# Router logits from x with scaled weights, h shared with GpSimd beside the top-k, and squares and fill work reordered

## What is computed

```python
h = rmsnorm(x) * gain * (1 + scale) + shift       # per channel; scale, shift differ for context and latent tokens
aff = softmax(h @ w_router)                       # over 16 experts
g, idx = top_k(aff.T, cap)                        # 16 context and 32 latent tokens for each expert
hid = silu(h[idx] @ w_gate) * (h[idx] @ w_up)
out = (hid @ w_down) * g                          # scattered back by idx
```

## Time and profile before

| | us |
|---|---|
| median of three runs | 2028.72 |
| lowest, highest | 2028.66, 2030.94 |
| the profiled execution, its own time | 2027.77 |
| its span in the profile | 2025.7 |
| PE busy | 1867.7 (92%) |
| DVE, ScalarE, GpSimd busy | 592.7, 341.0, 60.4 |
| HBM read | 546.91 MB |

### The profile page before, as it was taken

One profiled execution on the slowest core, in us unless ns is written; L12 is line 12 of the kernel. 1 busy time (PEld: TensorE's weight loads), 2 busy tenths in 40 slices (PEclk: granted clock), 3 DMA queues, 4 the chain that ended last, 5 costly groups with the idle time before them and its releaser, 6 DMA issues.

```text
span 2025.7 us, 19626 instructions
## 1 busy us (share of the span) xinstructions
PE 1867.7 (92%) x8214; PEld 938.6 (46%) x8214; DVE 592.7 (29%) x1160; ACT 341.0 (17%) x787; POOL 60.4 (3%) x47
## 2 busy tenths in 40 slices
PE   5999999999999988888789999999999998888886
PEld 2565556555544333233345655565555343333323
DVE  1232447545221111101132324654533102010102
ACT  4022331100211101000141322210003010100102
POOL 1100000000000000000030000000000000000000
PEclk9999999999999999999999999999999999999998
DMA  9322272442589999999972221716225999999995
GB/s 389 152 94 88 84 307 78 166 166 77 208 365 428 429 429 429 430 429 428 426 309 94 83 88 57 287 42 249 110 102 245 396 429 428 429 429 428 429 429 243
DMA packets 53544, 552.38 MB, mean 273 GB/s; under 512 B 5840, under 2 KB 10832, under 8 KB 12240
## 3 DMA queue, kind: packets, MB, share of 16 engines
q1 hardware_dynamic: 49680, 548.51, 65.2%
q10 hardware_dynamic: 3776, 2.62, 0.4%
HBM read 546.91 MB, written 4.19 MB: 272 GB/s over the span
## 4 chain that ended last, share of the span: by engine, by line
PE 65%; DMA 29%; DVE 3%; ACT 2%; issue 1%; POOL 0%; SPq 0%; POOLq 0%; DVEq 0%; ACTq 0%
PE psum L943 12%; DMA ring<-in_w_up 12%; PE psum L1115 12%; DMA ring<-in_w_down 12%; PE psum L802 11%; PE psum L1027 6%; PE psum L804 6%; PE psum L1040 4%; DMA wide<-in_w_gate 3%; PE psum L397 2%; DMA ring<-in_w_gate 2%; PE psum L862 1%; PE psum L765 1%; PE psum L1095 1%; PE psum L1163 1%
## 5 line engine op out<-in xcount | busy, mean ns | idle before, releaser
L943 PE MATMUL psum<-hT,ring 128*128 128x384 f32 x768 | 255.8, 486 | 0.0
L802 PE MATMUL psum<-hT,ring 128*128 128x384 f32 x720 | 244.4, 493 | 7.2 <-ACT dense L1295 5.1
L1115 PE MATMUL psum<-dense 128*64 128x512 f32 x864 | 195.4, 596 | 30.8 <-DMA dense<-in_w_up 17.6
L1115 PE MATMUL psum<-ring,dense 128*64 128x512 f32 x832 | 188.2, 596 | 26.9 <-DMA ring<-in_w_gate 16.0
L943 PEld LDWEIGHTS psum<-hT,ring 128*128 128x128 f32 x768 | 145.7, 190 | 100.9
L802 PEld LDWEIGHTS psum<-hT,ring 128*128 128x128 f32 x720 | 135.8, 193 | 96.5 <-issue 6.6
L1115 PEld LDWEIGHTS psum<-dense 128*64 128x64 f32 x864 | 62.5, 137 | 153.6 <-issue 129.1
L1027 PE MATMUL psum<-dense,ring 128*128 128x384 f32 x384 | 131.9, 487 | 0.0
L1805 DVE TENSOR_TENSOR state<-state,psum 128x512 f32<-128x512 f32 x32 | 22.0, 688 | 373.2 <-PE psum L1115 335.2
L804 PE MATMUL psum<-ring,hT 128*128 128x512 f32 x288 | 126.5, 592 | 0.0
L1115 PEld LDWEIGHTS psum<-ring,dense 128*64 128x64 f32 x832 | 59.8, 137 | 140.7 <-issue 119.1
(11 more groups left out here) (211 smaller groups left out, 1680.2 us busy)
## 6 DMA issues: line engine op xcount, KB each, us to landing
ring<-in_w_up SPq DMA_DIRECT2D x32, 2048.0 KB, 38.2
ring<-in_w_in SPq DMA_DIRECT2D x60, 1024.0 KB, 8.6
dense<-in_w_up SPq DMA_DIRECT2D x30, 2048.0 KB, 40.0
ring<-in_w_down SPq DMA_DIRECT2D x30, 2048.0 KB, 40.1
dense<-in_w_gate SPq DMA_DIRECT2D x24, 2048.0 KB, 35.6
wide<-in_w_down SPq DMA_DIRECT2D x20, 2048.0 KB, 40.2
ring<-in_w_gate SPq DMA_DIRECT2D x20, 2048.0 KB, 36.7
wide<-in_w_gate SPq DMA_DIRECT2D x20, 2048.0 KB, 38.1
```

The costliest lines, as they stand in the source:

```text
L802: last = M.matmul(psum[:, bank, 0:T], ring[:, n % RING, k, cols], hT[:, k, :], start=k == 0, stop=k == KD - 1)
L943: last = M.matmul(psum[:, Z[1], 0:T], ring[:, n_gate % RING, k, (j % 4) * P:(j % 4 + 1) * P], hT[:, k, :], start=k == 0, stop=k == KD - 1)
L1115: last = M.matmul(psum[HALF * half:HALF * (half + 1), bank, :], lhsT(k), w[:, kk, half * SLAB:(half + 1) * SLAB], start=k == 0, stop=k == ...
```

## The change

- Router: the logits are computed from xT and not from hT. DVE scales the router weights by the modulation's scale (router_scaled, one copy for context and one for latent columns). PE multiplies them with the chunks of xT, chunks 0 to 3 inside w_out (after group 5) and 4 to 7 after the norm sum; DVE multiplies the result by rs, which is the inverse norm of each token. The part of the logits that comes from the shift is made from w_r and modT (eight two-column products after group 1 of w_out), spread with a product with ones into PSUM, and the gather adds to it.
- The first chain fill moves from right behind w_out to behind the gathered logits. The other fills move behind the transposes of the affinities.
- h: DVE normalises chunks 0 to 2, between steps of the softmax. GpSimd normalises chunks 3 to 7 and applies scale and shift to chunks 6 and 7. ScalarE applies them to chunks 0 to 5, in between its reads of fills. The transposes of hT come in two halves (chunks 0 to 3, 4 to 7) after those of the affinities.
- Squares: three buffers, and GpSimd adds four chunks, not six. PE sums chunks 4 to 6 directly, then GpSimd's sum, then chunk 7. This holds for all five norm sums.
- Starts: in layer 0 w_in 0 is in ring slot 3 and modulation slab 3 in slot 0, half a z group comes before the transposes of modulation slab 1, and four z groups are begun ahead and not three. In layer 1 a modulation product comes before the norm sum, and two z groups are begun ahead.
- Decays: DVE computes their logarithms before rotation 2 and ScalarE makes the exponentials behind its reads of z groups 4, 5 and 6.
- keep_busy has 4 dummy products beside the top-k, where layer 0 had 8 and layer 1 had 18.

The core of the diff; context is cut, blocks are moved to the left, the semaphores' declarations are left out, and so are the decay blocks that only move.

```diff
-ADDED = 6
-DVE_MODULATES = ((3, 6, 7), (6, 7))
+ADDED = 4
+BEGUN = (4, 2)
+DVE_MODULATES = ((3, 6, 7), ())
+DVE_NORMS = 3
...
+router_scaled = flat(state1).rearrange("p (g k e) -> p g k e", g=2, k=KD)
+router_shift = w_r[:].rearrange("p k e -> p (k e)")[:, 0:NBLK * NE].rearrange("p (g e) -> p g e", g=NBLK)
...
-[("mod", 1, 1), ("modT", 1, 1), ("mod", 1, 3), ("modT", 1, 3)]]
+[("mod", 1, 1), ("mod", 1, 3), ("modT", 1, 1), ("modT", 1, 3)]]
...
-SLABS = [[("mod", j) for j in START_MODS[l]] + [("w_in", j) for j in range(9)] + [("mod", j) for j in DENSE_MODS[l]]
+FIRST_SLABS = [[("mod", 0), ("mod", 2), ("mod", 1), ("w_in", 0), ("mod", 3)], [("mod", 1), ("mod", 3), ("w_in", 0)]]
+SLABS = [FIRST_SLABS[l] + [("w_in", j) for j in range(1, 9)] + [("mod", j) for j in DENSE_MODS[l]]
          + [x for b in range(3) for x in (("w_in", 9 + 2 * b), ("branch", b), ("w_in", 10 + 2 * b))] + [("w_out", 0), ("w_out", 1)]
...
+load_half(0, 3, 0)
 wait_slab_free(sp, 0, 0)
-load_half(0, RING, 0)
-load_slab(0, 3)
-load_half(0, RING, 1)
+load_slab(0, RING)
+load_half(0, 3, 1)
...
-G.tensor_tensor(sum_sq, square[:, 0, :], square[:, 1, :], ALU.add).then_inc(sq_added, 2)
+G.tensor_tensor(sum_sq, squared[0], squared[1], ALU.add).then_inc(sq_added, 2)
 for k in range(2, ADDED):
     pool.wait_ge(sq_added, at(sq_added, mixer * ADDED + k))
     pool.wait_ge(sq_ready, at(sq_ready, mixer * KD + k + 1))
-    G.tensor_tensor(sum_sq, sum_sq, square[:, k % 2, :], ALU.add).then_inc(sq_added, 1)
+    G.tensor_tensor(sum_sq, sum_sq, squared[k % 3], ALU.add).then_inc(sq_added, 1)
...
 add_squares(layer, 1)
+pool.wait_ge(rs_ready, at(rs_ready, 2))
+for k in range(DVE_NORMS, KD):
+    G.tensor_tensor(hT[:, k, :], xT[:, k, :], rs[:], ALU.mult).then_inc(norm_pool, 1)
+for k in POOL_MODULATES:
+    pool.wait_ge(norm_pool, at(norm_pool, k - DVE_NORMS + 1))
+    for g, cols in enumerate((CTX, LAT)):
+        last = G.tensor_scalar(hT[:, k, cols], hT[:, k, cols], scale_ffn_all[:, layer, k, g:g + 1],
+                               modT_all[:, layer, 24 + k, g:g + 1], ALU.mult, ALU.add)
+    last.then_inc(h_pool, 1)
...
-pe.wait_ge(sq_added, count(sq_added, (mixer + 1) * ADDED))
-M.matmul(psum[:, bank, 0:T], ones, sum_sq, start=True, stop=False)
 for k in range(ADDED, KD):
+    if k == KD - 1:
+        pe.wait_ge(sq_added, count(sq_added, (mixer + 1) * ADDED))
+        M.matmul(psum[:, bank, 0:T], ones, sum_sq, start=False, stop=False)
     pe.wait_ge(sq_ready, count(sq_ready, mixer * KD + k + 1))
-    last = M.matmul(psum[:, bank, 0:T], ones, square[:, k % 2, :], start=False, stop=k == KD - 1)
+    last = M.matmul(psum[:, bank, 0:T], ones, squared[k % 3], start=k == ADDED, stop=k == KD - 1)
     last.then_inc(sq_summed, 1)
...
-    fill(START_FILL[0][1:6])
+    fill(START_FILL[0][1:5])
     z_first_half(0)
+    fill(START_FILL[0][5:6])
     z_first_half(1)
     fill(START_FILL[0][6:7])
     z_first_half(2)
     fill(START_FILL[0][7:8])
+    z_first_half(3)
 else:
+    fill(START_FILL[layer][0:1])
     norm_sum(TR[0], 0)
-    fill(START_FILL[layer][0:1])
+    fill(START_FILL[layer][1:2])
     z_first_half(0)
-    fill(START_FILL[layer][1:3])
+    fill(START_FILL[layer][2:4])
     z_first_half(1)
...
+def router_part(chunks):
+    pe.wait_ge(w_read, at(w_read, chunks[-1] + 1))
+    for g, cols in enumerate((CTX, LAT)):
+        for k in chunks:
+            q = k % 4
+            last = M.matmul(psum[32 * q:32 * q + 32, (O[0], TR[1])[g], cols], router_scaled[:, g, k, :], xT[:, k, cols], start=k < 4, stop=k >= 4)
+    return last
...
 for j in range(KD):
     if j % 4 == 0:
...
+    if j == 1:
+        pe.wait_ge(router_in, at(router_in, 16))
+        pe.wait_ge(mod2_ready, at(mod2_ready, 1))
+        pe.wait_ge(co_read, at(co_read, 4))
+        for k in range(KD):
+            q = k % 4
+            last = M.matmul(psum[32 * q:32 * q + 32, O[0], 0:2], w_r[:, k, :], modT_all[:, layer, 24 + k, :], start=k < 4, stop=k >= 4)
+        last.then_inc(shift_full, 1)
+    if j == 5:
+        pe.wait_ge(router_ready, at(router_ready, 2))
+        pe.wait_ge(shift_read, at(shift_read, 1))
+        router_part(range(4))
+norm_sum(TR[0], 1)
+router_part(range(4, KD)).then_inc(lgT_full, 1)
+pe.wait_ge(shift_ready, at(shift_ready, 3))
+M.matmul(psum[:, O[1], 0:NBLK * NE], ones, router_shift.rearrange("p g e -> p (g e)"), start=True, stop=False)
+pe.wait_ge(lgT_read, at(lgT_read, 2))
+for b in range(NBLK):
+    last = M.matmul(psum[:, O[1], b * NE:(b + 1) * NE], tmp[:, 1, b * P:(b + 1) * P], c_("gather_experts"), start=False, stop=b == NBLK - 1)
+last.then_inc(lg_full, 1)
 fill(CHAIN_FILL[layer][0:1])
-norm_sum(TR[0], 1)
-fill(CHAIN_FILL[layer][1:3])
-pe.wait_ge(router_in, at(router_in, 16))
-for k in range(KD):
...
-    last = M.matmul(psum[32 * q:32 * q + 32, TR[1], 0:T], w_r[:, k, :], hT[:, k, :], start=k < 4, stop=k >= 4)
-last.then_inc(lgT_full, 1)
-pe.wait_ge(lgT_read, at(lgT_read, 1))
-for b in range(NBLK):
-    last = M.matmul(psum[:, TR[0], b * NE:(b + 1) * NE], tmp[:, 1, b * P:(b + 1) * P], c_("gather_experts"), start=True, stop=True)
-last.then_inc(lg_full, 1)
-pe.wait_ge(w_read, at(w_read, KD))
-pe.wait_ge(z_read, f_of(*CHAIN_FILL[layer][2]) + 1)
-for n in range(2 * NBLK):
-    for q in range(4):
-        last = transpose(psum[:, H_BANKS[n], q * P:(q + 1) * P], hT[:, (n % 2) * 4 + q, (n // 2) * P:(n // 2 + 1) * P])
-    last.then_inc(hr_tr, 1)
 pe.wait_ge(aff_ready, at(aff_ready, 1))
 for b in range(NBLK):
     last = transpose(psum[0:NE, TR[1], b * P:(b + 1) * P], aff[:, b, :])
 last.then_inc(affT_full, 1)
+fill(CHAIN_FILL[layer][1:3])
+pe.wait_ge(w_read, at(w_read, KD))
+pe.wait_ge(z_read, f_of(*CHAIN_FILL[layer][2]) + 1)
+for half in range(2):
+    for k in range(4 * half, 4 * half + 4):
+        chunk_ready_wait(pe, layer, 1, k)
+    for b in range(NBLK):
+        for q in range(4):
+            last = transpose(psum[:, H_BANKS[2 * b + half], q * P:(q + 1) * P], hT[:, 4 * half + q, b * P:(b + 1) * P])
+        last.then_inc(hr_tr, 1)
 pe.wait_ge(hr_ev, at(hr_ev, 2))
-fill(CHAIN_FILL[layer][3:6])
+fill(CHAIN_FILL[layer][3:5])
 pe.wait_ge(hr_ev, at(hr_ev, 3))
-keep_busy((8, 18)[layer])
+keep_busy(4)
+fill(CHAIN_FILL[layer][5:6])
 pe.wait_ge(slots_ready, at(slots_ready, 2))
 for b in range(NBLK):
     last = transpose(psum[:, TR[0], b * NE:(b + 1) * NE], place[0:NE, b * P:(b + 1) * P])
 last.then_inc(slots_tr, 1)
+pe.wait_ge(hr_ev, at(hr_ev, 2 * NBLK))
 keep_busy(4)
-pe.wait_ge(hr_ev, at(hr_ev, 2 * NBLK))
...
-if 2 <= k < ADDED + 2:
-    sc.wait_ge(sq_added, at(sq_added, mixer * ADDED + k - 1))
-elif k >= 2:
-    sc.wait_ge(sq_summed, at(sq_summed, mixer * (KD - ADDED) + k - ADDED - 1))
+if 3 <= k < ADDED + 3:
+    sc.wait_ge(sq_added, at(sq_added, mixer * ADDED + max(2, k - 2)))
+elif k >= 3:
+    sc.wait_ge(sq_summed, at(sq_summed, mixer * (KD - ADDED) + k - ADDED - 2))
 elif first or layer:
     sc.wait_ge(sq_summed, at(sq_summed, mixer * (KD - ADDED)))
-A_.activation(square[:, k % 2, :], xT[:, k, :], ACT.Square).then_inc(sq_ready, 1)
+A_.activation(squared[k % 3], xT[:, k, :], ACT.Square).then_inc(sq_ready, 1)
...
 for k in range(first, last):
-    if k not in DVE_MODULATES[mixer]:
-        sc.wait_ge(norm_mul, at(norm_mul, mixer * KD + k + 1))
+    if k not in (POOL_MODULATES if mixer else DVE_MODULATES[0]):
+        if mixer and k >= DVE_NORMS:
+            sc.wait_ge(norm_pool, at(norm_pool, k - DVE_NORMS + 1))
+        else:
+            sc.wait_ge(norm_mul, at(norm_mul, mixer * KD + k + 1))
         for g, cols in enumerate((CTX, LAT)):
...
+read(START_FILL[layer][0:1])
...
-read(START_FILL[layer])
+read(START_FILL[layer][1:])
...
 for g in range(Z_FIRST):
     read_z(layer, g)
+    if g == 4:
+        decay_logs()
+    if g == 5:
+        decay_inside()
+    if g == 6:
+        decay_across()
...
-read(CHAIN_FILL[layer][0:1])
 inverse_rms(TR[0], 2)
-modulate(1, scale_ffn, 24)
-read(CHAIN_FILL[layer][1:3])
+modulate(1, scale_ffn, 24, 0, 1)
 sc.wait_ge(lg_max, at(lg_max, 1))
 A_.activation(aff, aff, ACT.Exp).then_inc(lg_exp, 1)
+read(CHAIN_FILL[layer][0:1])
+modulate(1, scale_ffn, 24, 1, 3)
+read(CHAIN_FILL[layer][1:2])
+modulate(1, scale_ffn, 24, 3, 4)
+read(CHAIN_FILL[layer][2:3])
+modulate(1, scale_ffn, 24, 4)
 sc.wait_ge(hr_tr, at(hr_tr, 2 * NBLK))
 for n in range(2 * NBLK):
     A_.activation(h_rows[:, n // 2, (n % 2) * 512:(n % 2 + 1) * 512], psum[:, H_BANKS[n], :], ACT.Copy).then_inc(hr_ev, 1)
-read(CHAIN_FILL[layer][3:6])
+read(CHAIN_FILL[layer][3:5])
 sc.wait_ge(stored, at(stored, 32))
 A_.preload_act_table(ACT.Silu)
+read(CHAIN_FILL[layer][5:6])
 def read_gathered(quad):
     for part in range(2):
...
+dve.wait_ge(router_in, at(router_in, 16))
+for g in range(2):
+    V.tensor_tensor(router_scaled[:, g], w_r[:], scale_ffn[:, :, g].unsqueeze(2).to_broadcast([P, KD, 32]), ALU.mult).then_inc(router_ready, 1)
 for j in range(KD):
+    if j == 4:
+        dve.wait_ge(shift_full, at(shift_full, 1))
```

(17 more changed lines are left out.)

120 lines of the change are left out of this document (67 added, 53 removed).

## The result

| | before | after |
|---|---|---|
| median, us | 2029.6 (2028.66 to 2030.94, 4 runs) | 2008.13 (2007.38 to 2009.07, 4 runs) |
| the profiled execution | 2027.77 | 2007.38 |
| its span | 2025.7 | 2005.6 |

A forecast was written before the change was run, and what follows sets the result against it. PE was taken to bound each layer through w_out, DMA transfers the experts. Terms -5.9 - 8.2 - 3.6 - 0.1 + 0.1 = -17.7 us gave 2011 us against the median of 2028.7, range 2004 to 2019.

The forecast's parts named there:

- Two regimes: Each layer: PE sets the pace from input projection to the end of w_out, DMA at 429 GB/s in the experts.
- Start of layer 0: Before w_out of layer 0: PE losses of 7.4 us go, norm sum costs 1.5 more; net -5.9 us (-3.5 to -7.4).
- Decays: Exponentials moved behind z groups 4 to 6: batches of at most 4.1 us hide under 5.6 us z groups, costed at nothing.
- Start of layer 1: Before w_out of layer 1: waits for GpSimd's adds and before z group 2 shrink; -8.2 us (-5 to -9).
- The end: Last norm sum: PE no longer waits 3.62 us for GpSimd's adds; -3.6 us (-2.5 to -3.8).
- Router stage, PE: From w_out's end W: 1.4 us inserted, logits at W + 6.1; PE's stage shrinks by 1.2 and 3.6 us.
- Router stage, transfers: Slab 3 issued 7.5 us later; DMA's 7.6 us pause only moves ahead of the slabs: -0.1 and +0.1 us.
- slack of the first expert product: Router stage: PE's first expert product may come 3.0 us (layer 0) and 5.6 us (layer 1) later before transfers wait.
- T's rule: Follow-up theory: an expert stage ends 450.7 us after slab 3's issue or 426.2 after slab 9's, whichever is later.
- rival 3: Router stage: GpSimd's tensor_scalar with SBUF scalars costs by the instruction, making the kernel slower, 2037 us; chance 0.03.
- Rival 1: Router stage is worth what PE gains, as transfers pause elsewhere or slabs need under 26 us: 2006 us; chance 0.12.
- GpSimd: Router stage: four tensor_scalar operations at 0.34 and 0.69 us, five multiplications at 1.0; up to 3 us DVE contention, sum unchanged.

The follow-up runs named there:

- experiment 1: The changed kernel with SP issuing expert slabs in the order 6, 7, 8, 3, 4, 5 instead of 6, 3, 7, 8, 4, 5: 2002.84 us, 2002.93 in a second series.
- experiment 4: The changed kernel with only the decays (DVE logarithms, ScalarE exponentials) put back ahead of the first reads of z groups: 2022.65 us.
- experiment 2: The kernel before with only SP's slab order changed to 6, 7, 8, 3, 4, 5 (the reordered twin): 2029.69 us, ratio 1.0003.
- experiment 3: The changed kernel with the router stage of before, keeping the new squares, norm sums, starts and decays: 2011.29 us.
- experiment 6: GpSimd's five multiplications of x by the inverse norm done twice: 2018.85 us in the changed kernel, 2017.54 us in it with slab order 6, 7, 8, 3, 4, 5.
- experiment 5: The kernel before with only the decay work of ScalarE and DVE moved behind the reads of z groups 4 to 6: 2021.05 us, ratio 0.9955.

## Why the prediction was right, step by step

**Two regimes.** Right, and it carried the result: all of the gain is at the seams where PE sets the pace, and the router stage gave +0.2 and 0.0 us, forecast -0.1 and +0.1.

**Start of layer 0**, forecast -5.9, measured -7.15 behind the landing of the first slab. That landing moved by 1.46 us more, but it is chance: one and the same kernel, that of experiment 1, had it at 14.99 and 13.42 in two traces, the three with the old start order at 14.68, 13.83 and 13.81, and those with the new one between 13.22 and 14.99. From the landing to w_out seven traces with the new start and five norm products have 481.3 to 482.7, 482.0 in the mean (experiment 4 is left out, which changes this stretch); before and its reordered twin have 488.4 and 488.1. So the change is worth 6.3 us here. The mis-sized term is the price of the two norm products: forecast 1.5 us, and the two kernels with three products have 481.0 in this stretch, so they cost 1.0. So the sum without that price, 7.4 us, came as 7.3. All three waits went and the clock stood at 1.00 in 42 to 46, where it was 0.57. z group 2 ended at 47.32, where I had said near 50: 1.5 us of that are the landing, and 1.25 the larger gain in this trace.

**Decays**, forecast at nothing once moved: right. In layer 1 the wait of 3.36 us is gone and no z group waits.

**Start of layer 1**, forecast -8.2, measured -8.36. That they agree within 0.2 us is partly luck, since the old start itself varies: the stretch before w_out of layer 1 took 492.39 us in before and 494.09 in its reordered twin, where the same wait of 3.4 us was followed by a lower clock (below). With the new start eight of nine traces have 484.01 to 484.03 (the ninth, 484.60, has the old squares), so the new start is worth 8.4 to 10.1 us here and in these traces its time hardly varies. What doesn't hang on luck is the order: played through, it gave the end of z group 2 at 1042.6 on before's scale; it came at 1033.96, which is 1042.4 with the 8.43 us by which layer 0 had ended earlier. The twin's z group 2 behind the wait (4.29 us in the earlier trace rows):

```profile
1045.40 5.49 PE L802 MATMUL psum<-hT,ring 128*128 128x384 f32 x8 [3.37 <-ACT dense L1295]
```

**The end**, forecast -3.6 (its own numbers, 2017.79 - 2014.1, give 3.7), measured -3.3: 0.15 us is a wait for the square of chunk 6, which I had as ready.

**Router stage, PE.** Inserted products 1.33 us, by the time from the start of w_out to W, 42.70 against 41.37 (forecast 1.4), logits W + 6.2 (6.1), copies until W + 18.5 (18.6), gather W + 21.8 (22.2) and in layer 1 W + 19.5 (19.7). **Router stage, transfers.** Slab 3 at W + 8.1 (8.0), no pause after it. The forecast that a pause of 7.6 us is only moved is what experiments 1, 2 and 3 confirm. One size was off: I put the slack of the first expert product at 3.0 and 5.6 us, and T's rule gives 1.6 and 4.0 (experiment 6 shows 1.8 and 4.1). So a slow GpSimd, rival 3, would have begun to cost over a microsecond earlier than I said. Rival 1, that the stage is worth what PE gains, did not come true, and it was one line of SP's order away: 2002.8 with the order of experiment 1, against its 2006.

**GpSimd.** The four tensor_scalar operations took 1.95 us, forecast 2.1, so rival 3 falls. That the total is so near is partly luck, the errors of the two sizes offset each other: 128 columns took 0.44 us and 256 took 0.55, where the forecast, in proportion to the columns, had 0.34 and 0.69. Its multiplications took 5.79 us for five, 1.19 us in the mean where the adds take 1.0. DVE's three normalisations took 0.86, 0.75 and 1.39 us beside them; in the kernel before, with GpSimd idle, the same form has a mean of 0.55 (line below). The Trainium skill (SBUF — State Buffer, Who interferes with whom) says that a DVE instruction with two SBUF inputs contends with a GpSimd instruction that reads SBUF; by that rule, the trace agrees in kind. Over the three it cost 1.35 us on DVE, and 0.36 more on the product that makes the affinities (0.57 us, 0.21 before), of the 3 that I allowed. It reached no path, as forecast.

The group of DVE in the kernel before, and that of GpSimd in the kernel after (count, busy us, mean ns, idle before):

```profile
L1557 DVE TENSOR_TENSOR hT<-xT,rs 128x384 f32<-128x384 f32 x32 | 15.5, 551 | 37.8 <-ACT rs L1259 37.8
```

```profile
L727 POOL TENSOR_TENSOR hT<-xT,rs 128x384 f32<-128x384 f32 x10 | 11.6, 1188 | 47.3 <-ACT rs L1305 47.3
...
L731 POOL TENSOR_SCALAR hT<-hT,scale_ffn,modT 128x128 f32<-128x128 f32 (+1 forms) x8 | 3.9, 496 | 0.0
```

**What the sum did not say.** The span moved by 20.1 us where the sum has 17.7. Of these 2.4 us the landing of the first slab has 1.46 and the rest of layer 0's start 1.25, of which only 0.4 stand in the mean of the traces; the other stretches give back 0.3. The medians moved by another 1.4 us, which is within the spread of single runs, 2.3 us before and 1.7 after. And the sum of separate parts holds for the change as a whole only: experiments 4 and 5 show 14.5 and 7.7 us for the same edit.

## What to carry to other kernels

When a path is shortened ahead of a stretch bound by transfers, look up which issue in the DMA queue follows from it, and what is queued behind that issue: here 5.3 us lay in one waiting entry that stood second and not fourth. State the end of such a stretch as the later of two issues, each plus its constant; here two traces gave the constants to half a microsecond, and the rest of the experiments could be read from the issues alone. And cost a wait of PE in a tuned kernel with what it does to the clock behind it, not with its length alone.
